# MLP second matrix: in two of eight K steps of seven 1024-column groups, seven block products in place of eight

## What is computed

```python
def sqrelu_mlp(x, w1, w2):
    return (jnp.square(jax.nn.relu(x @ w1)) @ w2).astype(x.dtype)

h = sqrelu_mlp(rmsnorm(x, norm_g[i, 2]), mlp_w1[i], mlp_w2[i])
x = x + rmsnorm(h, norm_g[i, 3])
```

## Time and profile before

| | us |
|---|---|
| median of three runs | 1794.78 |
| the profiled execution: its own time | 1794.94 |
| its span in the trace | 1792.9 |
| TensorE (matmul) busy in the span | 1786.5 |
| VectorE busy | 1120.4 |
| ScalarE busy | 817.8 |
| GpSimd busy | 115.6 |

### The profile page before, as it was taken

The page is one execution under the profiler, slowest core; times in us unless marked ns, Lnnn a source line. Parts: engine busy times, 40 slices in busy tenths (PEclk is TensorE's granted clock), DMA queues, the critical chain, the costliest instruction groups (busy, mean ns, idle before and its releaser), DMA issues.

```text
span 1792.9 us, 26965 instructions
## 1 busy us (share of the span) xinstructions
PE 1786.5 (100%) x8881; PEld 1514.9 (84%) x8881; DVE 1120.4 (62%) x1430; ACT 817.8 (46%) x1101; POOL 115.6 (6%) x162
## 2 busy tenths in 40 slices
PE   9999999999999999999999999999999999999999
PEld 7888888888888888888888887888888888888887
DVE  6567777556755665576556657755688655555654
ACT  6434444446433443344334445744444455554442
POOL 1012121000000000000000000100004011000000
PEclk9999999999999999999999999999999999999999
DMA  8564445545565555556555555565555555555554
GB/s 322 203 222 160 167 160 175 181 172 188 176 226 186 188 190 205 177 187 202 196 179 190 201 191 186 190 201 196 178 187 176 198 177 176 175 175 188 188 188 153
DMA packets 95060, 339.64 MB, mean 189 GB/s; under 512 B 11024, under 2 KB 11424, under 8 KB 94624
## 3 DMA queue, kind: packets, MB, share of 16 engines
q1 hardware_dynamic: 93392, 333.23, 54.7%
q0 software_dynamic: 752, 5.26, 0.8%
q10 hardware_dynamic: 864, 0.44, 0.1%
HBM read 336.77 MB, written 2.11 MB: 189 GB/s over the span
## 4 chain that ended last, share of the span: by engine, by line
PE 99%; DVE 1%; POOL 0%; ACT 0%; issue 0%; POOLq 0%; DVEq 0%
PE bank L434 57%; PE bank L413 23%; PE bank L418 12%; PE bank L484 1%; PE bank L450 1%; PE bank L563 1%; PE bank L604 1%; PE bank L619 1%; PE bank L610 0%; PE bank L603 0%; PE bank L620 0%; PE bank L534 0%; DVE w_lo L1271 0%; PE bank L477 0%; PE bank L629 0%; PE bank L760 0%
## 5 line engine op out<-in xcount | busy, mean ns | idle before, releaser
L1271 DVE TENSOR_TENSOR w_lo<-raw,w_hi 128x1024 fp32r<-128x1024 f32 x620 | 760.0, 1227 | 561.5 <-ACT w_hi L841 558.6
L841 ACT ACTIVATE w_hi<-raw 128x1024 fp32r<-128x1024 f32 x620 | 652.6, 1057 | 696.1 <-PE bank L434 511.2
L434 PE MATMUL bank<-w_hi,h_both 128*128 128x512 f32 x1544 | 479.9, 392 | 0.0
L434 PE MATMUL bank<-w_hi,a_both 128*128 128x512 f32 x1472 | 454.3, 390 | 0.0
L413 PE MATMUL bank<-h_both,w_hi 128*128 128x512 f32 x1792 | 432.6, 393 | 0.0
L413 PEld LDWEIGHTS bank<-h_both,w_hi 128*128 128x128 f32 x1792 | 330.4, 188 | 65.4
L434 PEld LDWEIGHTS bank<-w_hi,h_both 128*128 128x128 f32 x1544 | 287.8, 188 | 58.7
L434 PEld LDWEIGHTS bank<-w_hi,a_both 128*128 128x128 f32 x1472 | 275.4, 188 | 56.6
L434 PE MATMUL bank<-w_lo,h_both 128*128 128x512 f32 x772 | 300.8, 390 | 0.0
L434 PE MATMUL bank<-w_lo,a_both 128*128 128x512 f32 x736 | 286.4, 389 | 0.0
L418 PEld LDWEIGHTS bank<-h_both,w_lo 128*128 128x128 f32 x1792 | 229.7, 191 | 8.7
(11 more groups left out here) (190 smaller groups left out, 833.1 us busy)
## 6 DMA issues: line engine op xcount, KB each, us to landing
raw<-in_stream SPq DMA_DIRECT2D x622, 512.0 KB, 3.3
res<-in_x SPq DMA_DIRECT2D x4, 512.0 KB, 7.7
rowg<-in_norm_rows POOLq DMA_DIRECT2D x2, 1024.0 KB, 7.8
gate<-cum_rows POOLq DMA_DIRECT2D x1, 2048.0 KB, 7.8
out<-wide SPq DMA_DIRECT2D x8, 256.0 KB, 4.7
gate<-in_x_turned SPq DMA_DIRECT2D x5, 256.0 KB, 6.7
raw<-in_stream SPq DMA_DIRECT2D x3, 256.0 KB, 5.4
gate<-in_x_turned SPq DMA_DIRECT2D x1, 512.0 KB, 7.2
```

What stands on the lines that cost most here:

```text
L434: mm = pe.matmul(dst[t][:, :], xt[:, k0 + 2 * j + k, tt], wt[:, slot, w], start=j == 0 and k == 0 and n == 0, stop=last and k == 1 and n == 2)
L841: nc.scalar.activation(w_hi[:, slot, :], raw[:, slot, :], ACT.Copy).then_inc(hi_ready, 1)
L1271: nc.vector.tensor_tensor(w_lo[:, slot, :], raw[:, slot, :], w_hi[:, slot, :].bitcast(F32), ALU.subtract).then_inc(lo_ready, 1)
```

## The change

The second matrix of the MLP is worked in groups of 1024 output columns, seven of them (w = 0 to 6, two in each of passes 0 to 2 and one in pass 3); the last 1024 columns of pass 3 stay two groups of 512. A wide group has 16 chunks. A chunk now holds one K block of 128 rows and 1024 columns, again with 12 matmuls: token tile 0 with two column halves, then token tile 1 with two column halves. Two successive K blocks, two token tiles and two column halves make a 2 x 2 by 2 x 2 block product, eight products of three matmuls. At chunks 4 and 5 and at chunks 10 and 11 of each wide group (K pairs 4 and 6 of the hidden features) it is made with seven products after Strassen and Winograd (`seven_products`).

For this VectorE makes three sums of weight blocks (and one in place in `raw`), `outer_sums`, `inner_sum`, `last_sum`, and their low parts, `form_rest`; ScalarE makes their high parts, `form_hi`. Four sums of the hidden features are made in the tile stage (`x_forms`), with a high part on ScalarE and a low part on VectorE. Four of the products go to four other banks (`seven_bank`), three directly into banks of the plain sums (`plain_bank`), so a wide group holds all eight banks, and two successive groups swap the two sets. VectorE takes the four banks into the sums in SBUF between the rests of the last four chunks (`join_seven`), and the four plain banks (`plain_drain`) during the next group or ahead of the next tile stage. `wide_taken` counts the joins and the plain drains, one each for a group. The loops over the passes and groups are written out; the first four rounds of the tile stage of a pass stay a loop. The gain multiplications of the last pass, two behind each of three groups before, come six in a row behind the third.

```diff
+WIDE_CHUNKS = 16
+PAIR_ORDER = (0, 1, 4, 2, 3, 6, 5, 7)
+SEVEN_PAIRS = (4, 6)
+SEVEN_AT = (4, 10)
+WIDE_GROUPS = 7
...
+        plain_bank = [[bank[6], bank[7], bank[0], bank[1]], bank[2:6]]
+        seven_bank = [plain_bank[1], plain_bank[0]]
...
+            def product(dst, x_parts, w_parts, start=False, stop=False):
+                pe.matmul(dst[:, :], x_parts[0], w_parts[0], start=start, stop=False)
+                pe.matmul(dst[:, :], x_parts[1], w_parts[0], start=False, stop=False)
+                return pe.matmul(dst[:, :], x_parts[0], w_parts[1], start=False, stop=stop)
...
+            def wide_chunk(c, j, kt, plain, tiles_used):
+                first, last = j == 0, j == WIDE_CHUNKS - 1
+                pe.wait_ge(lo_ready, c + j + 1)
+                for t in range(NT):
+                    if first and t == 1 and tiles_used:
+                        for b in range(2):
+                            pe.wait_ge(tile_taken[b], tiles_used + 1)
+                    for n in range(2):
+                        mm = product(plain[2 * t + n], x_block(kt, t), w_block(j % RING, n), first, last)
+                    if last and t == 0:
+                        mm.then_inc(half_group_done, 1)
+                mm.then_inc(chunk_done, 1)
+            def seven_products(c, j, g, q, w, plain, seven):
+                kt = 2 * SEVEN_PAIRS[q]
+                slot = j % RING
+                first, last = q == 0, q == 1
+                pe.wait_ge(lo_ready, c + j + 1)
+                product(seven[0], x_block(kt, 0), w_block(slot, 0), first, last)
+                pe.wait_ge(x_form_ready, 2 * g + q + 1)
+                product(seven[1], x_form(q, 0), w_block(slot, 1), first, last).then_inc(chunk_done, 1)
+                pe.wait_ge(lo_ready, c + j + 2)
+                product(plain[0], x_block(kt + 1, 0), w_block(slot + 1, 0))
+                product(plain[1], x_form(q, 3), w_block(slot + 1, 1)).then_inc(chunk_done, 1)
+                pe.wait_ge(form_lo_ready, 2 * w + q + 1)
+                product(seven[3], x_form(q, 2), w_form(1), first, last)
+                product(seven[2], x_form(q, 1), w_form(0), first, last)
+                product(plain[2], x_block(kt + 1, 1), w_form(2)).then_inc(forms_done, 1)
+            def wide_group(g, n):
+                c = FIRST["mlp"] + g * 64 + 32 + 16 * n
+                w = 2 * g + n
+                plain, seven = plain_bank[n], seven_bank[n]
+                if w:
+                    pe.wait_ge(wide_taken, 2 * w - 1)
+                for j in range(0, WIDE_CHUNKS, 2):
+                    pair = PAIR_ORDER[j // 2]
+                    if n == 0:
+                        hidden_in(g, 2 * pair + 1)
+                    if j in SEVEN_AT:
+                        if w:
+                            pe.wait_ge(wide_taken, 2 * w)
+                        else:
+                            for b in range(2):
+                                pe.wait_ge(group_taken[b], 6)
+                        seven_products(c, j, g, SEVEN_AT.index(j), w, plain, seven)
+                        continue
+                    for k in range(2):
+                        wide_chunk(c, j + k, 2 * pair + k, plain, g * 8 + 20 if n == 0 else 0)
...
+            pe.wait_ge(wide_taken, 2 * WIDE_GROUPS - 1)
+            group(c + 48, 0, 5, a_hi, a_lo)
+            pe.wait_ge(wide_taken, 2 * WIDE_GROUPS)
+            last_group(c + 56, 5, 2, a_hi, a_lo)
...
+                    if b == 1 and isinstance(i, int) and i in SEVEN_PAIRS:
+                        q = SEVEN_PAIRS.index(i)
+                        act.wait_ge(x_form_step, 4 * (2 * g + q) + 4)
+                        if g:
+                            act.wait_ge(forms_done, 4 * g)
+                        nc.scalar.activation(x_form_hi[:, q, :, :], x_form_raw, ACT.Copy).then_inc(x_form_hi_ready, 1)
...
+            def wide_splits(g, n):
+                c = FIRST["mlp"] + g * 64 + 32 + 16 * n
+                w = 2 * g + n
+                for j in range(WIDE_CHUNKS):
+                    ahead = j + RING
+                    if ahead in SEVEN_AT:
+                        act.wait_ge(form_step, 4 * (2 * w + SEVEN_AT.index(ahead)) + 2)
+                    next_split(c + j)
+                    if ahead - 1 in SEVEN_AT:
+                        step = 2 * w + SEVEN_AT.index(ahead - 1)
+                        act.wait_ge(form_step, 4 * step + 4)
+                        if step:
+                            act.wait_ge(forms_done, step)
+                        nc.scalar.activation(form_hi[:, :, :], form_raw, ACT.Copy).then_inc(form_hi_ready, 1)
+                    if j == SEVEN_AT[1] + 1:
+                        act.wait_ge(forms_done, 2 * w + 2)
+                        nc.scalar.activation(form_sum2, seven_bank[w % 2][0][:, :], ACT.Copy).then_inc(form_hi_ready, 1)
...
+                    if b == 1 and isinstance(i, int) and i in SEVEN_PAIRS:
+                        x_forms(g, SEVEN_PAIRS.index(i))
                     rest(c_b + 1, 2 * b + 1)
-                    if isinstance(i, int) and b == 0:
+                    if b == 1 and isinstance(i, int) and i in SEVEN_PAIRS:
+                        q = SEVEN_PAIRS.index(i)
+                        dve.wait_ge(x_form_hi_ready, 2 * g + q + 1)
+                        nc.vector.tensor_tensor(x_form_lo[:, q, :, :], x_form_raw, x_form_hi[:, q, :, :].bitcast(F32),
...
+            def x_forms(g, q):
+                step = 4 * (2 * g + q)
+                a11, a21 = [relu2[0][:, t * P:(t + 1) * P] for t in range(NT)]
+                a12, a22 = [relu2[1][:, t * P:(t + 1) * P] for t in range(NT)]
+                s1, s2, s3, s4 = [x_form_raw[:, f, :] for f in range(4)]
+                nc.vector.tensor_tensor(s1, a21, a22, ALU.add).then_inc(x_form_step, 1)
+                nc.vector.tensor_tensor(s3, a11, a21, ALU.subtract).then_inc(x_form_step, 1)
+                dve.wait_ge(x_form_step, step + 1)
+                nc.vector.tensor_tensor(s2, s1, a11, ALU.subtract).then_inc(x_form_step, 1)
+                dve.wait_ge(x_form_step, step + 3)
+                nc.vector.tensor_tensor(s4, a12, s2, ALU.subtract).then_inc(x_form_step, 1)
...
+            def outer_sums(step, c, slot):
+                for s in range(2):
+                    dve.wait_ge(raw_landed[slot + s], 16 * (c // RING) + 16)
+                b11, b12, b21, b22 = w_blocks(slot)
+                nc.vector.tensor_tensor(form_raw[:, 1, :], b22, b12, ALU.subtract).then_inc(form_step, 1)
+                nc.vector.tensor_tensor(b12, b12, b11, ALU.subtract).then_inc(form_step, 1)
+            def inner_sum(step, slot):
+                b11, diff, b21, b22 = w_blocks(slot)
+                dve.wait_ge(form_step, 4 * step + 2)
+                nc.vector.tensor_tensor(form_raw[:, 0, :], b22, diff, ALU.subtract).then_inc(form_step, 1)
+            def last_sum(step, slot):
+                b11, diff, b21, b22 = w_blocks(slot)
+                dve.wait_ge(form_step, 4 * step + 3)
+                nc.vector.tensor_tensor(form_raw[:, 2, :], b21, form_raw[:, 0, :], ALU.subtract).then_inc(form_step, 1)
+            def form_rest(step):
+                dve.wait_ge(form_hi_ready, 3 * (step // 2) + step % 2 + 1)
+                nc.vector.tensor_tensor(form_lo[:, :, :], form_raw, form_hi[:, :, :].bitcast(F32),
+                                        ALU.subtract).then_inc(form_lo_ready, 1)
...
+            def plain_drain(w, t, n):
+                c = FIRST["mlp"] + (w // 2) * 64 + 32 + 16 * (w % 2)
+                if t == 0:
+                    dve.wait_ge(half_group_done, GROUPS_BEFORE["mlp"] + w + 1)
+                else:
+                    dve.wait_ge(chunk_done, c + WIDE_CHUNKS)
+                add_scaled(w, t, n, plain_bank[w % 2][2 * t + n][:, :]).then_inc(ff_sum_ready, 1)
+                if t == 1 and n == 1:
+                    dve.wait_ge(ff_sum_ready, 4 * w + 4)
+                    dve.sem_inc(wide_taken, 1)
+            def join_seven(w, part):
+                p1, p5, p6, p7 = [b[:, :] for b in seven_bank[w % 2]]
+                base = 8 * w
+                if part == 0:
+                    dve.wait_ge(form_hi_ready, 3 * w + 3)
+                    nc.vector.tensor_tensor(form_sum, form_sum2, p6, ALU.add).then_inc(join_step, 1)
+                    add_scaled(w, 0, 0, p1).then_inc(join_step, 1)
+                elif part == 1:
+                    dve.wait_ge(join_step, base + 1)
+                    add_scaled(w, 0, 1, form_sum).then_inc(join_step, 1)
+                    nc.vector.tensor_tensor(form_sum2, form_sum, p7, ALU.add).then_inc(join_step, 1)
+                elif part == 2:
+                    dve.wait_ge(join_step, base + 4)
+                    add_scaled(w, 0, 1, p5).then_inc(join_step, 1)
+                    add_scaled(w, 1, 1, p5).then_inc(join_step, 1)
+                else:
+                    add_scaled(w, 1, 0, form_sum2).then_inc(join_step, 1)
+                    dve.wait_ge(join_step, base + 6)
```

(71 more changed lines are left out.)

196 lines of the change are left out of this document (107 added, 89 removed).

## The result

The changed kernel takes 1801.15 us, median of seven runs (1800.53 to 1801.59), against 1794.86 us for the kernel before beside it. The ratio is 1.0035 with a 95% interval of 1.0023 to 1.0046: slower by 6.3 us. The profiled execution took 1801.59 us, its span is 1799.9 us.

A forecast was written before the change was run, and what follows sets the result against it. TensorE's unbroken matmuls were taken to bound the kernel, with VectorE's order deciding where it waits. 1794.94 - 9.5 + 10.0 + 6.8 + 0.3 = 1802.5 us for the profiled execution, 1802.4 us for the median, range 1796 to 1809.

The forecast's parts named there:

- What is removed: TensorE in seven wide groups: two steps each, three matmuls fewer per step, 42 x 0.2267 = 9.5 us saved.
- Wait 1, the join: Wide group ends: TensorE waits for join part 3, queued behind a rest needing chunk 14; 7 x 1.43 = 10.0 us.
- E: The end of a wide group's last matmul, from which the forecast counted the join's times; TensorE released at E + 1.43.
- my 0.28: Release after the join's additions: VectorE waits 0.15 us for its own result, then the signal to TensorE.
- Wait 2, the last tile: First wide group of a pass, before its seventh matmul: waits for the last tiles' drain, 4 x 1.7 = 6.8 us.
- The delay of 0.65 us: Tile stage: sums and low part for the forms, two tiles earlier, make the last sum 0.55 to 0.85 us late.
- What stays covered: Other places in groups and tiles, tightest chunk 8 with 0.9 us margin: together 0 to 3 us, taken as 0.3.
- 38 of 42.2 us: VectorE's predicted busy time in a wide group: 15 us added to the 23 us of before, so it fits.
- Shorter waits: Rival: releases overlap and the tiles' delay is gone, 7 x 1.2 + 4 x 0.8 = 11.6 us, so 1797 us; 15%.
- No wait: Rival: the join is over before the group's last matmul ends, the whole 9.5 us comes through, 1785.3 us; 8%.
- VectorE falling behind as a whole: Rival: chunk 8 and form parts late in each step, 14 x 0.6 = 8 us more, about 1811 us; 7%.
- The clock: Rival: TensorE's clock falls to 1.2 GHz for a chunk behind eleven pauses, 30 us more, about 1832 us; 2%.

The follow-up runs named there:

- the pair of kernels with seven and eight products: Eight products in every step, no join, in the changed kernel's structure with token tile 0 worked first: 1794.57 us; its partner with seven products and reordered engines: 1785.02 us.
- the kernel with more sums: Changed kernel plus four extra VectorE subtractions into unused places, 0.8 us, ahead of the fourth sum of hidden features: 1803.08 us, one run.
- the kernel with token tile 0 first: Changed kernel, with the first two chunks of each pass's first wide group worked token tile 0 of both, then token tile 1 of both: 1799.63 us.
- the kernel without waits: Changed kernel with all three orders: join ahead of chunk 14's rest, token tile 0 of two chunks first, second step's outer sums behind two rests: 1785.02 us.
- longer join: Changed kernel with two more sums of 512 columns, 0.6 us each, ahead of the join's last two scaled additions: 1815.6 us, one run.
- join behind the last chunk: Changed kernel with part 3 of the join moved behind the rest of slot 3, which waits for the group's last chunk: 1832.6 us, one run.

## Why the prediction was right

It said 1802.4 us in a range of 1796 to 1809, slower by more than 0.2%; the kernel takes 1801.15.

**What is removed:** 42 matmuls, 9.5 us. Right; 8839 are in the page, and the pair of kernels with seven and eight products differs by 9.5 us.

**Wait 1, the join:** 7 x 1.43 = 10.0 us said, 4 x 1.35 + 3 x 1.61 = 10.2 us found. The steps came out one by one: the rest at E - 1.40 (885.43 with E at 886.85: -1.42), the additions over at E + 1.15 (+1.13). The release was smaller than my 0.28: VectorE's wait for its own result and the signal to TensorE overlap, 0.11 us from the end of the additions to the matmul, and then 0.11 on the second matmul. What I had not seen is the 0.26 us of the loop start. I had argued from the earlier trace rows that loops cost TensorE nothing; that holds as long as TensorE's queue is not held by a wait. The two errors nearly cancelled, 0.6 us against 0.8. Moving the join either way moved the waits as worked out, so this step is shown.

**Wait 2, the last tile:** the wait is there, but 4 x 0.98 = 3.9 us, not 6.8. This is the term that was mis-sized. The part without the forms was 1.07 and fits. The delay of 0.65 us that I let the forms leave at the last tile was nil. The timeline of the changed kernel, two tiles earlier, shows why:

```profile
835.69 0.42 DVE L1689 TENSOR_TENSOR a_both<-gate,a_both 128x256 fp32r<-128x256 f32 x1 [0.48 <-ACT a_both L1171]
836.03 0.28 DVE L1708 TENSOR_TENSOR wide<-gate 128x128 f32<-128x128 f32 x1
...
836.96 1.22 DVE L1388 TENSOR_TENSOR w_lo<-raw,w_hi 128x1024 fp32r<-128x1024 f32 x1
838.10 0.68 DVE L1697 TENSOR_TENSOR x_form_lo<-wide,x_form_hi 128x512 fp32r<-128x512 f32 x1
838.70 1.22 DVE L1388 TENSOR_TENSOR w_lo<-raw,w_hi 128x1024 fp32r<-128x1024 f32 x1
```

The tile ended at 832.47, so the low part of the features starts 3.22 us behind it, not 3.55 as in the earlier trace rows. In the tiles that are written out VectorE waits 0.48 us for the high part, inside a loop 0.73 to 0.82 us; the trace of before had both, and I took the row from a loop. This one is written out, in pass 0 of the kernel before:

```profile
467.83 0.42 DVE L1572 TENSOR_TENSOR a_both<-gate,a_both 128x256 fp32r<-128x256 f32 x1 [0.48 <-ACT a_both L1079]
```

With that and 0.93 us in place of 1.1 for the four sums, the next tile's rest (838.70) is 0.33 us late. The rest behind it (843.93) has 0.5 us of idle time ahead of it in the undisturbed tiles and 0.18 here, so it is on time again. In the kernel with more sums the delay was 1.13 us and 0.53 of it reached the last tile: a delay above this slack does arrive.

The rule that I cited from the Trainium skill (VectorE: DVE Perf Modes, section The TRN2 errata) for 128 columns, 291 ns, held: the four sums took 284 to 293 ns. By the same rule (1536 + 151) / 0.96 = 1757 ns is an estimate for the low part of the forms, and the changed kernel has 1753.

**What stays covered:** I took 0.3 us and named chunk 8 as the tightest place; it is 1.05 us in pass 0 and nothing elsewhere. In pass 2 the margin was 0.4 us in place of 0.9, and the reason is wait 2: chunk 8 was ready at 21.6 us, as I said, but TensorE wanted it at 22.2 and not at 22.7, since wait 2 was over 0.6 us sooner. That 21.6 came out by luck. My terms, 15.2 and 3.3 us and 2.5 for two sums and a rest, add up to 21.0; the load began at 14.5 and landed not 3.3 us later but 4.6 (the idle time above, 4.4 to 5.0 in the seven groups). The median of the earlier trace rows is over all loads; here two are issued within 2 us, and whether that is why was not tried. Where the waits before chunk 8 are shorter still, the place costs more, as the kernel with token tile 0 first showed.

**The sum.** The waits are 15.2 us where I had 17.1: 2.9 less for wait 2, 0.2 more for wait 1, 0.75 more for chunk 8. That the forecast lies only 1.25 us above the median is in part luck: the first is largely offset by the other two and by the 0.6 us that these waits leave open in the medians. VectorE's load was too high in my sum as well: 38 of 42.2 us in a wide group were said, 35.5 are in the kernel without waits.

**The rivals.** *Shorter waits* had one half right, no delay of the tiles at the last one (4 x 0.98 where it had 4 x 0.8); its other half, 1.2 us at each join, did not come. *No wait* (1785.3 us) is what the best order gives, 1785.0 us: the price was right and the order decides. VectorE falling behind as a whole is refuted by the same kernel. The clock stayed at 1.00 in the changed kernel behind its waits of 1.0 to 1.6 us, and fell only in the kernels whose waits are 2.5 us and more. The rule of the Trainium skill that I had weighed for this stands in its page TensorE: Matmul & The Clock Gate, in the section A second HAM failure mode: psum-queue depth-cycling, not in the one that I named. The changed kernel shows nothing of what it speaks of (1.00 throughout the groups), the two with longer waits do (0.50 behind seven and behind four waits).

## What to carry to other kernels

When an engine's order is written by hand, read for each release what the instruction ahead of it waits for. Here two scaled additions took 1.4 us with 6.7 us of VectorE free in each group (42.2 less 35.5), and cost 9.5 us over seven groups because they stood behind an instruction that could start only 1.4 us ahead of the group's end. Put what frees a buffer ahead of what waits for the consumer's latest progress, and put what waits for a load behind everything whose data are already there. And when one such wait is removed, look at once for the next in the same order: 2.4 of 3.9 us came back one place later until that was reordered too.

## What the runs showed of the hardware

- The granted clock after a pause of TensorE: behind waits of 1.0 to 1.6 us it stayed at 1.00 in eleven of eleven places (the changed kernel), also behind one of 1.9 us (token tile 0 first); behind 2.5 to 2.8 us it fell to 0.50 in four of seven (longer join); behind 3.95 to 4.3 us in seven of seven (join behind the last chunk), and was back 3 to 6 us after TensorE had begun again. A pause of 4 us cost an estimated 1.4 to 2.9 us more than itself: 3 to 6 us of matmuls at 0.43 in place of 0.23 us. The kernels with these longer waits ran once each.
- The start of the tile loop on TensorE cost nothing where no wait stood ahead of it (no gap in the earlier trace rows, nor in the kernel with all three orders) and 0.26 us behind a wait (1.61 us, against 1.35 with the loop written out).
- A VectorE instruction in a loop, which finds its place from the loop's counter, began 0.25 to 0.34 us later behind the same ScalarE result than the same instruction written out (0.73 to 0.82 against 0.48 us of waiting, in the kernel before and in the changed one). This was read from the traces and not tried by itself.
